# A decoder layer on one core: the matmuls of the V stage cut from 512 columns to 256, two sums to a PSUM bank

## The reference, cut to what matters

```
u = jnp.take(expert_u, eb, axis=0)
act = jax.nn.gelu(jnp.einsum('tkd,td->tk', u, xb), approximate=False)
v = jnp.take(expert_v, eb, axis=0)
return jnp.einsum('tk,tkd->td', gb * act, v)
```

## Time and profile before

| | |
|---|---|
| executions shown | 2186.41, 2191.9, 2196.75 us, median 2191.9 |
| the profiled execution: its own time | 2189.96 us |
| its span | 2188.1 us |
| TensorE busy with matmuls in the span | 2084.0 us, 95%, 13326 matmuls |
| V stage, first to last start of a matmul | 1453.20 to 2169.77 us |

### The profile page before, as it was taken

How to read it: one execution, slowest core, us unless ns; L and a number is a source line. 1 busy time by engine, 2 the same in 40 slices (tenths; PEclk the granted TensorE clock), 3 DMA queues, 4 the chain that set the end, 5 groups by cost and what they waited for, 6 DMA issues and landing times.

```text
span 2188.1 us, 36961 instructions
## 1 busy us (share of the span) xinstructions
PE 2084.0 (95%) x13326; PEld 1863.6 (85%) x13326; DVE 1149.4 (53%) x1835; ACT 904.8 (41%) x1144; POOL 1101.1 (50%) x450
## 2 busy tenths in 40 slices
PE   8797898988989999999999999999999999999996
PEld 6686787877989999999999999998888888888885
DVE  7578557043255991266666665025454544445455
ACT  6332334363533433543333333444444444444443
POOL 6675666874776898887777777870000000000001
PEclk9898999999999999999999999999999999999998
DMA  8443545663654655655555555566665655666663
GB/s 310 125 144 116 173 135 175 191 194 98 215 169 130 194 166 166 191 182 164 161 161 162 161 162 163 185 225 214 183 191 185 189 184 190 187 186 188 186 189 117
DMA packets 104754, 383.32 MB, mean 175 GB/s; under 512 B 12144, under 2 KB 12656, under 8 KB 103408
## 3 DMA queue, kind: packets, MB, share of 16 engines
q1 hardware_dynamic: 101232, 365.50, 53.6%
q10 hardware_dynamic: 3456, 16.89, 2.1%
HBM read 378.15 MB, written 4.19 MB: 175 GB/s over the span
## 4 chain that ended last, share of the span: by engine, by line
PE 61%; POOL 24%; issue 14%; DVE 1%; POOLq 0%; ACT 0%; DVEq 0%; ACTq 0%
POOL wlo L353 24%; PE ps L1179 20%; PE ps L1181 20%; PE ps L1180 20%; PE ps L1462 2%; POOLq L352 0%; DVE x_back L1134 0%; DVE stats L619 0%; ACT big L593 0%; DVE stats L1145 0%; POOLq L356 0%; DVE big L1139 0%; ACT x_back L600 0%; PE ps L1488 0%; POOLq L353 0%
## 5 line engine op out<-in xcount | busy, mean ns | idle before, releaser
L353 POOL TENSOR_TENSOR wlo<-raw,whi 128x1024 fp32r<-128x1024 f32 x444 | 1095.2, 2470 | 375.3 <-ACT whi L403 371.0
L403 ACT ACTIVATE whi<-raw 128x1024 fp32r<-128x1024 f32 x436 | 461.6, 1060 | 818.7 <-PE ps L1181 817.7
L1179 PE MATMUL ps<-xh,whi 128*128 128x256 f32 x2432 | 696.0, 286 | 20.1 <-POOL wlo L353 10.5
L1180 PE MATMUL ps<-xl,whi 128*128 128x256 f32 x2432 | 683.3, 281 | 0.0
L1181 PE MATMUL ps<-xh,wlo 128*128 128x256 f32 x2432 | 683.1, 281 | 0.0
L1106 DVE TENSOR_TENSOR wlo<-raw,whi 128x1024 fp32r<-128x1024 f32 x248 | 303.9, 1225 | 350.1 <-ACT whi L551 350.1
L1179 PEld LDWEIGHTS ps<-xh,whi 128*128 128x128 f32 x2432 | 461.4, 190 | 22.4 <-POOL wlo L353 10.9
L1180 PEld LDWEIGHTS ps<-xl,whi 128*128 128x128 f32 x2432 | 466.6, 192 | 0.1
L1181 PEld LDWEIGHTS ps<-xh,wlo 128*128 128x128 f32 x2432 | 460.9, 190 | 0.0
L551 ACT ACTIVATE whi<-raw 128x1024 fp32r<-128x1024 f32 x256 | 271.6, 1061 | 404.1 <-PE ps L1181 404.1
L1179 PE MATMUL ps<-whi,gate_hi 128*128 128x512 f32 x1024 | 406.9, 397 | 0.0
(11 more groups left out here) (184 smaller groups left out, 1432.6 us busy)
## 6 DMA issues: line engine op xcount, KB each, us to landing
raw<-in_w_u SPq DMA_DIRECT2D x256, 512.0 KB, 3.5
raw<-in_w_v SPq DMA_DIRECT2D x256, 512.0 KB, 3.5
raw<-in_w_front SPq DMA_DIRECT2D x180, 512.0 KB, 3.6
big<-in_x_t ACTq DMA_DIRECT2D x4, 512.0 KB, 9.2
big<-in_x ACTq DMA_DIRECT2D x4, 512.0 KB, 5.3
big<-in_mem ACTq DMA_DIRECT2D x4, 512.0 KB, 6.2
big<-in_mem_t ACTq DMA_DIRECT2D x2, 1024.0 KB, 6.0
big<-in_x ACTq DMA_DIRECT2D x2, 1024.0 KB, 6.1
```

The costliest lines, as they stand in the source:

```text
L353: nc.gpsimd.tensor_tensor(wlo[:, j % SPL, :], raw[:, j % RAW, :], whi[:, j % SPL, :], ALU.subtract).then_inc(lo_done, 1)
L403: nc.scalar.activation(whi[:, j % SPL, :], raw[:, j % RAW, :], ACT.Copy).then_inc(hi_done, 1)
L1179: nc.tensor.matmul(out_ap, sh, mh, start=start, stop=False)
L1180: nc.tensor.matmul(out_ap, sh, ml, start=False, stop=False)
```

## The change

`v_products` walks over four stretches of 256 columns where it walked over two of 512. A stretch of 256 columns of output is one half of a bank, so two open sums lie in each of the eight banks. The three matmuls are written out in place of the helper, with the two high-by-something ones first as before. `start` is set only for the even stretch of a bank, on its first use; the odd stretch begins without it. Number formats, values, order of the adds for each output, waits, loads and splits are those of before.

```
             def v_products(s, g, half, tb, first=False, last=False):
 
-                for c in range(2):
-                    t = slice(tb * P, (tb + 1) * P)
-                    cols = slice(c * 512, (c + 1) * 512)
-                    ins = three(ps[:, 4 * tb + 2 * half + c, :], gate_hi[:, g, t], gate_lo[:, g, t], whi[:, s, cols],
-                                wlo[:, s, cols], first, last)
+                t = slice(tb * P, (tb + 1) * P)
+                for c in range(4):
+                    cols = slice(c * 256, (c + 1) * 256)
+                    out = ps[:, 4 * tb + 2 * half + c // 2, c % 2 * 256:(c % 2 + 1) * 256]
+                    opens = first and c % 2 == 0
+                    nc.tensor.matmul(out, gate_hi[:, g, t], whi[:, s, cols], start=opens, stop=False, skip_group_check=True)
+                    nc.tensor.matmul(out, gate_hi[:, g, t], wlo[:, s, cols], start=False, stop=False, skip_group_check=True)
+                    ins = nc.tensor.matmul(out, gate_lo[:, g, t], whi[:, s, cols], start=False, stop=last, skip_group_check=True)
                 return ins
```

## The result

The change moved the time by +0.3%: 2197.21 us (median of 20, 2193.16 to 2203.25) against 2190.16 (median of 20, 2186.21 to 2197.18), ratio 1.003 with a 95% interval of 1.0021 to 1.004. It is a small loss, 4.6 to 8.8 us, clear of zero and within the half per cent. 2198.8 had been forecast.

A forecast was written before the change was run, and what follows sets the result against it. TensorE was taken to bound the kernel's V stage. 6144 matmuls at 117.8 ns against 716.8 us gave +6.9 us, other parts nothing: 2191.9 + 6.9 = 2198.8 us, range 2168 to 2207.

The forecast's parts named there:

- TensorE bounds the stage one for one: V stage: everyone waits for TensorE, so a changed distance between its matmuls changes the time one for one.
- 2.3 ns a cut: V stage: cutting one 512-column matmul in two costs 2.3 ns, 3072 times, +6.9 us.
- The pace comes in with the U stage's stream: The untouched U stage enters the V stage at 117.8 ns per 256-column matmul, and the V stage keeps it.
- the long pace: TensorE's longer step, 117.8 ns at 256 columns, 233.3 at 512; expected in the new V stage, chance 0.62.
- the short pace: TensorE's shorter step, 113.3 ns at 256 columns, 228.9 at 512.
- The argument from the third tile of `w_in`: Front stage: the form with weights streamed also ran at the long pace when cut to 256 columns, 117.7 ns.
- No cost for two sums in a bank: V stage: stretch changes that now stay inside a bank cause no stall, at nothing.
- the rival of a late load: V stage: a change inside a bank costs 0.08 us, 1024 times, +84 us, 2283 us; chance 0.10.
- Splits, loads and supply hidden: V stage: splits, loads and the supply of TensorE instructions keep up with the matmuls, at nothing each.
- The short pace as a rival: The new V stage runs at 113.3 ns, 20.7 us shorter, 2171.2 us, -0.9%; chance 0.20.
- The load as the bound: V stage: loads of 189 ns cannot overlap and set the step, +444 us, 2636 us; chance 0.02.

The follow-up runs named there:

- experiment 4: Four float32 transposes in the U stage, after the last gate products: changed kernel 2165.97 us, one piece on 2168.02 us; kernel before 2174.76 us.
- experiment 5: Zero-adding float32 products ahead of 20 V-stage passes, changed kernel: 2206.72 us; transposes ahead of the V stage plus zero-adding bf16 products, kernel before: 2175.81 us.
- experiment 2: Changed kernel with its four stretches in the order 0, 2, 1, 3, so the bank changes each time: 2196.68 us, ratio 1.0027.
- experiment 1: Four float32 transposes between the U and V stages: kernel before 2178.37 us, ratio 0.9948; changed kernel 2197.84 us, ratio 1.0045.

## Why the prediction held, point by point

- **TensorE bounds the stage one for one.** Shown: +6.95 us of stage, +7.05 us between the medians (4.6 to 8.8 by the interval), PE busy for all 715 us. That 2198.8 was 1.6 us too high is the median it started from: 2191.9 of three executions, 2190.16 of twenty.
- **233.3 ns and 117.8 ns, hence 2.3 ns a cut.** Shown: 117.8 measured, +6.9 forecast for the stage, +6.95 found.
- **The pace comes in with the U stage's stream.** Right, and now shown by experiment 4, where a pace set some 30 pieces ahead goes over into the V stage in both forms. Its origin, too, is where I put it: behind gate products the U stage goes at the long pace in all 14 profiles, with the short pace ahead of the first and the long one ahead of the others. What experiment 5 refutes is the wider rule that I made of it, by the kind of matmul alone. The argument from the third tile of `w_in` was weaker than it looked: it has 117.8 ns in 13 of the 14 profiles and 113.4 in the execution of 2174.75 us of experiment 4, with the same code.
- **No cost for two sums in a bank.** For the change of half it is shown, by experiment 2 and by the steps of the changed kernel, none over 122 ns; the rival of a late load there has no room. That two open sums cost nothing by themselves rests on the equal step of the late U stage.
- **Splits, loads and supply hidden.** ScalarE and VectorE wait 6.6 and 6.8 us longer than before and PE for nobody.
- **The short pace as a rival.** It did not occur in the 20 executions of the changed kernel, whose fastest took 2193.16 us against the 2171.2 that it would give. It is real all the same: with it, the changed kernel takes 2166 to 2168 us, and then the sign of the change turns. In the profiles the V stage is some 7 us shorter with 256 columns than with 512 (6144 x 113.3 = 696 against 3072 x 228.9 = 703), since 2 x 113.3 is 2.3 ns less than 228.9. The medians, 2165.97 and 2174.76, say the same with 8.8 us, though their intervals touch.
- **The load as the bound.** Not at 256 columns. At 128 it nearly doubles the stage, if it is the load.

What stays open is what selects a pace. It is chosen where a stream resumes, is kept until the stream is broken or the clock falls, and goes over from form to form: in ten profiles without a break the V stage took over the pace of the U stage, five times the long and five times the short one. Where other matmuls broke a stream of the U or the V stage, the same break in the same form came out the same way each time, with the pace ahead taken into account. Four transposes left the V stage's 256-column form long and its 512-column form, like the U stage, short. Behind idleness or a stretch at half the clock, the same place came out both ways. No run here says why.

## What to carry to other kernels

Where TensorE bounds a stage, read the step from start to start and not the duration; a steady step can have two values for the same instructions, and a few matmuls placed elsewhere may change it for hundreds of microseconds. Cutting a matmul of 512 fp32r columns in two of 256 costs or gains 1% of its stage depending on that step, and two sums in one bank took nothing here; cutting once more nearly doubled the stage. When an edit comes out within 10 us, compare the steps of the untouched stages first: they alone can move the time by as much.

## What was not expected of the hardware

- Two steady steps for each size of fp32r matmul at the same granted clock: 113.3 and 117.8 ns for 256 columns, 228.9 and 233.3 for 512, both kept without a single step out of line for up to 700 us.
- Four float32 transposes, 0.4 us of work, made the kernel before 12 us faster (experiment 1), and in the U stage 14 us, and the changed kernel 31 us (2197.21 to 2165.97). That last one is the fastest version of this study, 1.06% under the kernel before.
- Matmuls of 128 fp32r columns start 111.7 ns apart, hardly closer than those of 256, and four-byte ones of 64 columns 108 on average.
- With an idle time of 2.6 us ahead of each pass, the granted clock was at 1.2 GHz for a while in 14 of 20 passes, and none of these came back from there at the short pace. In the U stage of the kernel before, at 834 us, a stream did: its next 719 matmuls start 113.3 ns apart.
